# Loading the input projection's weights through fp32 staging buffers, cast on two engines, with the output weights' loads released at once

## The reference, cut to what matters

```python
z = _rms(x, norm_w) @ w_in            # w_in: 1024 x 2304, fp32 in memory
# z -> q (512) | k (128) | v (128) | g_a (512) | u (512) | g_p (512)
q = _rms(q, q_norm_w); k = _rms(k, k_norm_w)
attn_o = _sink_attn(q, k, v, ...)     # window of 128 keys, blocks of 128 queries
pool_o = _pool(u, ...)                # trailing means over 2/4/8/16, then w_pool
mixed = concat([attn_o * silu(g_a), pool_o * silu(g_p)])
y = x + mixed @ w_out                 # w_out: 1024 x 1024
```

## Time and profile before

| | kernel before |
|---|---|
| median of 3 runs | 381.25 us |
| the profiled execution's own time | 380.0 us |
| its span on core 4, the slowest | 378.0 us |
| spans of the 8 cores | 374.9 to 378.0 us |
| TensorE busy | 297.6 us |
| ScalarE, VectorE, POOL busy | 165.7, 163.3, 81.2 us |
| moved by the DMA engines | 38.43 MB |

### The profile page before, as it was taken

How to read it: one execution, slowest core, us unless ns; L and a number is a source line. 1 busy time by engine, 2 the same in 40 slices (tenths; PEclk the granted TensorE clock), 3 DMA queues, 4 the chain that set the end, 5 groups by cost and what they waited for, 6 DMA issues and landing times.

```text
span 378.0 us, 5873 instructions; the slowest of 8 cores (374.9 to 378.0 us)
## 1 busy us (share of the span) xinstructions
PE 297.6 (79%) x1839; PEld 143.9 (38%) x1865; DVE 163.3 (43%) x276; ACT 165.7 (44%) x332; POOL 81.2 (21%) x84
## 2 busy tenths in 40 slices
PE   0135768899777899985879999986789999868893
PEld 0024333333343344443434344443333444645341
DVE  0406265210588723017756422226572215728842
ACT  1515367533978522244555621165754224663110
POOL 8000001440013346000113613001162400104510
PEclk9999697999969999997666999997899999855899
DMA  7999999990030000995820024330000304300145
GB/s 180 273 229 151 224 175 208 179 163 1 2 118 2 2 3 1 194 243 118 233 91 1 3 79 144 111 125 2 0 3 0 111 10 178 101 7 2 63 159 179
DMA packets 23404, 38.43 MB, mean 102 GB/s; under 512 B 5951, under 2 KB 15455, under 8 KB 23327
## 3 DMA queue, kind: packets, MB, share of 16 engines
q1 hardware_dynamic: 8207, 30.06, 25.0%
q0 software_dynamic: 15168, 8.00, 18.2%
HBM read 37.38 MB, written 11.21 MB: 129 GB/s over the span
## 4 chain that ended last, share of the span: by engine, by line
PE 50%; ACT 13%; DVE 11%; issue 11%; DMA 11%; POOL 2%; DVEq 0%; ACTq 0%; SPq 0%; POOLq 0%
PE B L467 29%; PE B L663 11%; DMA win<-w_in 7%; ACT PT L566 3%; PE B L588 3%; DMA xb<-xh 2%; DVE PT L577 2%; PE B L559 2%; ACT lnb L483 2%; ACT lnb L481 2%; DMA xr<-xh 2%; DVE rden L604 2%; PE B L596 2%; DVE qTn L485 2%; DVE ysb L675 1%
## 5 line engine op out<-in xcount | busy, mean ns | idle before, releaser
L467 PE MATMUL B<-hT,win 128*128 128x512 bf16 (+2 forms) x749 | 176.8, 348 | 24.7 <-DMA win<-w_in 11.1
L467 PEld LDWEIGHTS B<-hT,win 128*128 128x128 bf16 x768 | 68.1, 103 | 103.8 <-issue 52.4
L663 PE MATMUL B<-wout,mixT 128*128 128x512 bf16 x251 | 75.7, 379 | 1.6 <-DVE oT L609 1.0
L611 POOL TENSOR_TENSOR mixT<-oT,sga 128x512 bf16<-128x512 f32 x16 | 21.9, 1371 | 166.1 <-DVE oT L609 152.7
L675 DVE TENSOR_TENSOR ysb<-B,xr 128x512 f32<-128x512 f32 (+1 forms) x34 | 23.1, 687 | 49.6 <-PE B L663 34.7
L566 ACT ACTIVATE PT<-B 128x512 bf16<-128x512 f32 x64 | 35.6, 594 | 18.6 <-PE B L559 13.7
L577 DVE TENSOR_TENSOR PT<-PT,cstb 128x512 bf16<-128x512 bf16 x60 | 33.1, 570 | 23.2 <-ACT PT L566 22.2
L454 PE MATMUL B<-cstb,hn 128*128 128x128 bf16 (+1 forms) x144 | 20.9, 241 | 21.5 <-DVE hn L450 14.5
L663 PEld LDWEIGHTS B<-wout,mixT 128*128 128x128 bf16 x256 | 24.5, 97 | 30.9 <-issue 4.8
L450 DVE SCALAR_TENSOR_TENSOR hn<-xb,st,nwb_s 128x1024 bf16<-128x1024 f32 (+1 forms) x18 | 23.0, 1280 | 22.5 <-ACT st L448 22.5
L559 PE MATMUL B<-qTn,kTn 64*128 64x256 bf16 x128 | 20.7, 317 | 12.5 <-ACT PT L566 9.1
(11 more groups left out here) (109 smaller groups left out, 270.0 us busy)
## 6 DMA issues: line engine op xcount, KB each, us to landing
xb<-xh SPq DMA_DIRECT2D x17, 512.0 KB, 8.3
xr<-xh SPq DMA_DIRECT2D x16, 512.0 KB, 5.1
y<-ysb SPq DMA_DIRECT2D x16, 512.0 KB, 3.3
win<-w_in POOLq DMA_DIRECT2D x9, 512.0 KB, 37.8
wout<-w_out POOLq DMA_DIRECT2D x8, 256.0 KB, 11.6
nks<-ck SPq DMA_DIRECT2D x1, 1016.0 KB, 13.7
nvs<-cv SPq DMA_DIRECT2D x1, 1016.0 KB, 9.9
nwb_s<-nwb SPq DMA_DIRECT2D x1, 512.0 KB, 5.6
```

Of the source, the lines that this page charges most:

```text
L467: S.add("pe", lambda e, k=k, b_=b_: e.matmul(B[b_][:, 0:T], win[:, k, j * 128:(j + 1) * 128], hT[hT_slot][:, k, 0:T], start=(k == 0), stop ...
L611: S.add("pool", lambda e: e.tensor_tensor(out=mixT[:, 0:4, q0:q0 + 128], in0=oT[:].rearrange("p (c q) -> p c q", c=4), in1=sga[:, :, q0:q0 ...
L663: S.add("pe", lambda e, nh=nh, m=m, bk=bk: e.matmul(B[bk][0:rows, :], mx[:, m, col0:col0 + rows], wout[:, m, nh * 512:(nh + 1) * 512], sta ...
```

## The change

It replaces `load_w_in` and takes two dependencies away.

w_in now comes in 16 pieces of 128 rows (one k) by 1152 columns (half a, then half b), fp32, 590 KB each, issued by SP. They land in three staging slots in turn, which are the buffers `sga`, `sgp` and `uT`, not otherwise in use before tile 0's projections. Each piece is cast to bf16 into `win`, the even ones on VectorE, the odd ones on ScalarE, and a slot is loaded again only after its cast. A matmul of row block k waits for the piece that holds its k and half: a for column tiles 0 to 8, b for 9 to 17. The transfers of w_out and w_pool lose the gate; they are still cast by POOL's transfers, and their costs in the planner become 6 + 4m and 40. The halo and the tiles are computed as before.

```diff
         def load_w_in():
-            for gi, (j0, j1) in enumerate(WGROUPS):
-                for j in range(j0, j1):
-                    wg_of[j] = f"wing{gi}"
-                S.add("pool", lambda e, j0=j0, j1=j1: e.dma_start(out=win[:, :, j0 * 128:j1 * 128],
-                                                                 in_=w_in_v[:, :, j0 * 128:j1 * 128]),
-                      w=[f"wing{gi}"], dma=f"wing{gi}", c=3.0 + gi * 5.0)
+            slots = [(sga[:].rearrange("p c t -> p (c t)"), ["sga"]),
+                     (sgp[:].rearrange("p c t -> p (c t)"), ["sgp"]),
+                     (uT[:].rearrange("p g t -> p (g t)"), ["uT0", "uT1", "uT2", "uT3", "uTh"])]
+            n = 0
+            for k in range(8):
+                for hh in range(2):
+                    sv_t, res = slots[n % 3]
+                    sv = sv_t[:, 0:1152]
+                    c0 = hh * 1152
+                    S.add("sp", lambda e, sv=sv, k=k, c0=c0: e.dma_start(out=sv, in_=w_in[k * 128:(k + 1) * 128, c0:c0 + 1152]),
+                          w=res, dma=f"wstg{n % 3}", nb=128 * 1152 * 4)
+                    wr = [f"win{k}{'ab'[hh]}"]
+                    if n % 2 == 0:
+                        S.add("dve", lambda e, sv=sv, k=k, c0=c0: e.tensor_copy(out=win[:, k, c0:c0 + 1152], in_=sv),
+                              r=res, w=wr, c=0.75)
+                    else:
+                        S.add("act", lambda e, sv=sv, k=k, c0=c0: e.activation(out=win[:, k, c0:c0 + 1152], in_=sv,
+                                                                              func=AF.Copy), r=res, w=wr, c=CA(1152))
+                    n += 1
 
         def load_late_weights():
             w_out_v = w_out.rearrange("(m p) c -> p m c", p=128)
             stgB = [ysb[0][:], ysb[1][:], xr[0][:]]
             resB = ["ysb0", "ysb1", "xr0"]
-            gate = [f"wing{len(WGROUPS) - 1}"]
             for m in range(8):
                 S.add("pool", lambda e, m=m: e.dma_start(out=wout[:, m:m + 1, :], in_=w_out_v[:, m:m + 1, :]),
-                      r=gate, w=[f"wout{m}"], dma=f"wout{m}", c=50.0 + 3.0 * m)
+                      w=[f"wout{m}"], dma=f"wout{m}", c=6.0 + 4.0 * m)
             S.add("pool", lambda e: e.dma_start(out=wpool[:], in_=w_pool.rearrange("g c d -> c g d")),
-                  r=gate, w=["wpool"], dma="wpool", c=45.0)
+                  w=["wpool"], dma="wpool", c=40.0)
@@ inproj
-                      r=[wg_of[j], f"hT{hT_slot}"], w=[f"B{b_}"], c=CP(T))
+                      r=[f"win{k}{'a' if j < 9 else 'b'}", f"hT{hT_slot}"], w=[f"B{b_}"], c=CP(T))
```

## The result

The changed kernel takes 421.59 us in the median (419.92 to 423.03), the kernel before 381.20 in the same series (379.43 to 382.17). The ratio is 1.106, with a 95% interval of 1.104 to 1.108: slower by 40 us. The forecast of 396 had the sign right and 25.6 us too little, and the range, up to 409, does not hold the time.

What follows compares the result with a forecast made beforehand. The start was taken as bound by transfers, the rest mostly by TensorE. From 380.0 us, 26 us of later front less 10 us given back made 396 us; the range was 382 to 409.

Steps and rivals of the forecast that it cites:

- What bounds the kernel: Whole kernel: the start is bound by transfers with full DMA engines, the rest mostly by TensorE.
- The order of transfers: SP's queue at the start: 11 x blocks and others stand ahead of the last w_in piece, 17.2 MB together.
- w_in usable at 75: Start: shared transfers and the last cast make w_in usable at 75 us; ends of the term 50 and 85.
- the rival of the handshake: Start: w_in pieces wait for casts or cache copies on SP's queue; usable at 85, total 406 us; chance 0.16.
- The 11.4 us saved: w_in load: taking 9.44 MB to the hardware queue saves 11.4 us of engine time, the change's gain.
- From w_in to the dense tiles in 20.4 us: After w_in is usable: halo's projections 3 us, then tile 0's 17.4 us, before the 12 dense column tiles.
- k, then q0 and q2 in rounds of 8 matmuls: Tile 0's projections: k 3.4 plus chain 3.5, then q0 and q2 at 5.2 each, 10.5; sum 17.4 us.
- Given back, 10 us: After tile 0's projections: 10 us of the 26 us delay is recovered, 4 by (a) and 6 by (b).
- (a): After tile 0's projections: earlier-planned pool groups and output blocks fill TensorE's idle time; 0 to 8 us, 4 taken.
- (b): Attention 1: caches no longer move between 147 and 195 us; 0 to 10 us gained, 6 taken.
- The gaps for w_out: Start: w_out rides in gaps left by SP's waits; w_in usable at 61, total 382 us; chance 0.12.
- the faster one: Start: large packets run fast, little software queue gets in; w_in usable at 55, total 370 us; chance 0.14.

Runs made afterwards that it cites:

- experiments 1 and 2: Experiment 1 has its own line; 2: changed kernel with only the two cache loads put behind the last w_in pieces, 409.57 us, ratio 1.080.
- experiment 1: Changed kernel with w_out and w_pool gated behind w_in at old costs: 397.36 us; kernel before, ungated with new costs: 380.59 us.

## Why the prediction was right in sign and wrong in size

**What bounds the kernel** held. The start is bound by transfers, and by the sharing of engines between the queues (experiments 1 and 2).

**The order of transfers** held as worked out: the profile has 11 x blocks in front of the last piece, and 17.18 MB on SP's queue.

**w_in usable at 75** failed: it was 88.0. The chip's terms are 18.55 MB at 72.4% of 88 us = 63.7 us, and 31.2% = 27.5 us of software queue, 91.2 in all, over an overlap of 1.036. I had 54.0 and 23.5 over 1.08, and 3.2 of start and cast. The difference by terms:
- 17.18 MB at 3.43 us per MB (63.7 / 18.55) instead of 3.14: 58.9 instead of 54.0, 4.9 us. The rate of the earlier trace rows was a mean over a run with mostly quiet engines. With the other queue silent it was 3.26 (90.2% of 62 us over 17.18 MB). The Trainium skill, "DMA: Bandwidth & Descriptors", section "Bandwidth", gives about 358 GB/s per core with both cores of a pair streaming; the full stretch shows 291, and the measurement decides.
- All cache packets went beside w_in, not two thirds: 4.0 us. The issue of ckb at 36.5 us shows it:

```profile
36.50 1.16 POOL L442 DMA_DIRECT2D ckb<-ck  x1 [29.51 <-DMA wout<-w_out]
```

- With the caches there so early, the copies to the outputs follow right behind the last piece on SP's queue and run beside it: 18.55 - 17.18 = 1.37 MB, 4.7 us. In the rival of the handshake I had them ahead of a piece; they did their harm from behind.
- The overlap of 1.036 instead of 1.08 adds 3.0 (77.5 / 1.036 less 77.5 / 1.08).

(4.9 + 4.0 + 4.7) / 1.036 + 3.0 less the 3.2 that the shares already hold is 12.9, against 13.0 measured. The 11.4 us saved by not casting on the way are engine time, yet in experiment 1 w_in came only 3.2 us earlier than before. Its one queue filled the engines to 90.2%, where the old stream had 107.9%. That three slots are the reason is not shown: no run has the fourth slot together with the gate.

**From w_in to the dense tiles in 20.4 us** failed worst as a step: 117.85 - 88.0 = 29.9. The halo took 4.3 (I had 3), tile 0 25.5 (I had 17.4). "k, then q0 and q2 in rounds of 8 matmuls" was wrong: the order has k with v, q0 with q1 and q2 with q3, so three rounds of 16 matmuls and a chain, 6.9, 7.6 and 11.1 us here; the last has q3's chain behind q2's, with 8 matmuls of g_a between them. The reason that I gave for the 30.0 us before, late x blocks, does not hold. In the changed kernel no engine waits for an x block there, and tile 0 needs 4.5 us less; but its matmuls are busy for 4.4 us less (19.20 and 14.79, at clocks of 0.79 and 0.93): what it gained is the clock, and its 10.8 us outside the matmuls are those of before (10.9). Those rounds are in the old trace as well; I had read the stretch's waits, and should have counted its rounds.

**Given back, 10 us**: 6.2. (a) is 0, not 4: between marks 0 and 1 the gap is 62.9 instead of 62.6. The pool groups weren't moved to a place where they help; POOL waits for oT as in the earlier trace rows, and the first output matmul is again 55 us behind the mark:

```profile
L675 PE MATMUL B<-wout,mixT x250: 376/379/389, 173.1 to 411.3; 128*128 128x512 bf16 x125
```

```profile
154.83 1.27 POOL L623 TENSOR_TENSOR mixT<-oT,sga 128x512 bf16<-128x512 f32 x1 [22.06 <-DVE oT L621]
```

(b) held: 7.7 us between marks 1 and 2 (I took 6), and the old kernel with early caches shows it alone (gap 74.2 instead of 83.2), but at the price of 4.3 us in the gap before, where the caches then move. The last stretch is 1.4 longer.

**The sum**: 13.0 + 9.5 + 3.8 = 26.3 on spans, for 420.2 - 378.0 - 16 = 26.2 found.

**The rivals.** The handshake: 85 by its condition and 88 in fact, but only in small part by its mechanism; a fourth slot makes w_in usable 5.4 us earlier and takes off 6 to 7 us of 40. The gaps for w_out (usable at 61) and the faster one (usable at 59 or less) are out: even with nothing on the software queue w_in is usable at 62.0.

**Where the 40 us are**, taken off one by one in this order: caches 12.0, w_out and w_pool 12.2 (397.4), a halves first 6.7 (390.7), `uT` freed 4.7 (386.0), the costs 6.4 (379.6). By the ratios, which leave out the differences between series, they are 10, 14, 5, 5 and 6. The parts aren't additive: the fourth and third together are 20 us where the gate is missing. What is left against the old kernel with the same costs (375.8) is 3.8 us, so that with every repair tried staging still doesn't pay. Why is open; that mark 0 comes at 74.2 there and at 69.4 in the old kernel fits it. Open too is why the old kernel without its gate (380.6) doesn't gain what it gains with short costs (375.8), though its caches go out at 83.9 as well. Its marks 0, 1 and 2 are at 70.6, 138.9 and 214.4, the other's at 69.4, 136.3 and 210.5, so it falls back by little more than 1 us in each stretch; the planner's order differs in both and I didn't part them.

## What to carry to other kernels

A load that the first work waits for is priced by all that shares the DMA engines until it lands: here a gate on later loads moved it forward by nearly as many microseconds as these loads took (13.8 for 14.6). When the order of arrival is changed, ask which operation needs the last piece, and which early operation writes a buffer now lent to staging. Before calling a stretch late because of a transfer, count its rounds of banks and chains.

## What the runs showed of the hardware

- SP can stand in the issue of a transfer with many small rows: 17.62 us for the third of three pieces of 1024 rows of 1 KB, 2.34 for the second and 0.43 for the first, with nearly nothing in flight, against 0.33 us for 128 rows of 4.6 KB.
- The hardware queue with all 8 cores loading needed 3.26 us per MB alone and 3.43 beside the software queue, where the shares of the two sum to 1.04.
- VectorE's cast of 1152 columns from fp32 took 0.76 us, where the row of 640 columns gave 1.24; ScalarE took 1.16 for the same:

```profile
80.36 0.76 DVE L426 CAST win<-uT 128x1152 bf16<-128x1152 f32 x1 [3.28 <-DMA uT<-w_in]
```
